# Cross-attention scores as three fp32r products, and another grouping of the FFN's columns with a ninth paired column, in a one-core decoder layer

## The chip, the cores and the metric

The kernel runs on one core of a Trainium2 chip. The metric is the device time of one execution in microseconds. Three runs of the kernel before gave 868.54, 869.44 and 870.27 us; the median is 869.44 us. Lower is better.

## What is computed

One layer of a causal decoder, for 512 prompt tokens and 8 samples of 4 tokens (544 token columns in all), model width 1024, all in fp32:

```python
gb, gc, u, q, k, v = split_mix(rmsnorm(x, norm_mix_w) @ w_in)       # conv mixer and differential attention
x += concat(conv_mixer, diff_attention) @ w_out
mk, mv = memory_kv(mem, norm_mem_w, w_ckv)                          # 256 memory tokens, 4 heads of 256
q = (rmsnorm(x, norm_cross_w) @ w_cq).reshape(b, t, 4, 256)
s = einsum('bqhd,bkhd->bhqk', q, mk) * 256 ** -0.5                  # the scores over the memory
x += einsum('bhqk,bkhd->bqhd', softmax(s), mv) @ w_co
up = rmsnorm(x, norm_ffn_w) @ w_up                                  # 1024 -> 2 * 2816: gate half and up half
c = causal_dwconv(up, prefix, conv_w, conv_b)                       # width 3, per channel
x += (silu(c[..., :2816]) * c[..., 2816:]) @ w_down                 # 2816 -> 1024
y = rmsnorm(x, norm_final_w)
```

## The kernel before

Activations lie transposed: 128 channels on the partitions, tokens along the row. `x` is 8 such k-tiles of 544 columns. An fp32 product is made of three fp32r products: each operand is split into a high part (ScalarE, a copy to fp32r) and a low part (VectorE, the operand minus its high part), and high x high, high x low and low x high are added in one PSUM bank. For weights these are `w_hi` (L1531, a ring of 3) and `w_lo` (L1867, a ring of 4, like the raw weights `w_raw` that the DMA brings, L870). The split of tile n + 3 can begin on ScalarE only when tile n is done (`split_hi`, L1524 to L1532), and the load of tile n + 4 is issued when tile n is done.

**A tile** is one block of 128 output channels: for `k` k-tiles, 3 matmuls for each half of 272 tokens, so 6 matmuls per k-tile (L1180). Its result lies in one of two PSUM pairs, `proj0` or `proj1` by the parity of its number, and tile n may start only when the result of tile n - 2 has been taken out (`wait_tile_out`, L1158).

**Order.** `make_schedule` (L164) writes one list of steps. Each engine walks the same list and issues its own part of each step, in that order, and an engine that waits in one step holds all its later steps up.

**Cross attention.** Eight query tiles (`cq`) fill `qc_t`. Then come eight units `c_score` (two pairs of heads by four token blocks). A unit is 4 matmuls of two fp32 operands, `mk_t` and `qc_t`, 128x256 each (L1431; the trace shows each as two instructions). VectorE takes the maximum (L2258), ScalarE the exponential (L1744), VectorE scales by the reciprocal (`c_mix`, L2265 and L2268), and TensorE transposes (`c_turn`, L1273), one unit behind the scores. Between them stand value tiles (L1136) and the sample group's work. The step `cq_blocks`, just behind the first `c_score`, concerns GpSimd alone.

**FFN.** There are 22 columns of 128 channels. An unpaired column is a gate tile and an up tile of 8 k-tiles each, 96 matmuls. A paired column computes both with 7 products (`prod`, r = 1, 2, 5, 6, 7, 3, 4, in that order) instead of 8, each 12 matmuls, 84 in all (L1262 to L1264); the weight sums that it needs are made on VectorE (`sums`, L2069 to L2073) and split in three parts (`pair_split`, L2082). Paired are 5, 7, ... 19, eight columns. For each column VectorE then scales (`up_in`, L2021), applies the convolution (`taps`; its first tap is ScalarE's, L1789, the other two L2030 and L2032), multiplies by the gate (`gate`, L2037, L2039), ScalarE splits off the high part (L1798) and VectorE the low part (`act`, L2043). Down tiles sum the columns of a group into `x` (`add`, L1999); the groups are columns 0-3, 4-7, 8-11, 12-15 and 16-21, and the down tiles of a group stand two each beside the first four columns of the next group. The last group's eight down tiles have 6 k-tiles each; the first two are begun (`half_tile`) with all k-tiles but the last. Behind each of them ScalarE squares the result and applies the final norm's weight, and VectorE adds the squares up. The last tile is done half by half (`last_half`), and the final norm follows.

In what follows d(g, n) is down tile n of the group g, counted from 0.

## Time and profile before

| | us |
|---|---|
| median of three runs | 869.44 |
| the profiled execution, its own time | 869.0 |
| the span of its trace | 867.2 |
| TensorE busy | 848.2 (98%) |
| VectorE busy | 553.9 (64%) |
| ScalarE busy | 364.2 (42%) |
| mean granted TensorE clock | 0.995 |

The span runs from the first to the last instruction; the profiled execution took 1.8 us more than it. TensorE's busy time counts a matmul until its modelled end, so consecutive matmuls overlap, and what one costs is read from the distance between the starts. L numbers are lines of the kernel.

### The profile page before, as it was taken

How to read it: one execution, taken by the hardware profiler on the slowest of the kernel's cores; microseconds unless marked ns; L12 is line 12 of the kernel's file. 1: busy time of each engine (PE TensorE's matmuls, PEld its weight loads, DVE VectorE, ACT ScalarE, POOL GpSimd, SP SyncE). 2: the span in 40 equal slices, each digit the busy share in tenths (PEclk: the TensorE clock that was granted, in tenths of full speed). 3: DMA queues.
4: the chain of work that ended last, by engine and by line, in shares of the span. 5: the costliest groups of instructions: out<-in, count | busy, mean ns of one | idle time of the engine just before them, and what ended most of it. 6: DMA issues, size and time to landing. Idle time of an engine off the chain costs nothing.

```text
span 867.2 us, 17354 instructions
## 1 busy us (share of the span) xinstructions
PE 848.2 (98%) x6884; PEld 798.8 (92%) x6884; DVE 553.9 (64%) x981; ACT 364.2 (42%) x652; POOL 76.9 (9%) x149
## 2 busy tenths in 40 slices
PE   7999999999999999999999999999999999999994
PEld 6988877789999999877899999999999999999994
DVE  6444246678584633465454899679688796796754
ACT  7302143366453711354333665345254353452452
POOL 2320000000000000000000331101012011010200
PEclk9999999999999999999999999999999999999998
DMA  8898699731233465579134222233223322332223
GB/s 309 264 366 293 211 328 328 243 99 43 57 99 119 149 243 180 184 282 375 49 114 133 87 74 73 85 105 95 86 82 89 120 75 84 112 96 66 77 73 104
DMA packets 50146, 131.25 MB, mean 151 GB/s; under 512 B 5939, under 2 KB 8503, under 8 KB 49810
## 3 DMA queue, kind: packets, MB, share of 16 engines
q1 hardware_dynamic: 48064, 124.40, 43.6%
q0 software_dynamic: 1712, 5.62, 1.8%
q8 instruction: 55, 0.90, 0.4%
q14 instruction: 25, 0.20, 0.1%
q10 hardware_dynamic: 290, 0.12, 0.1%
HBM read 123.12 MB, written 7.00 MB: 150 GB/s over the span
## 4 chain that ended last, share of the span: by engine, by line
PE 82%; DVE 1%; DMA 1%; issue 1%; ACT 0%; SPq 0%; DVEq 0%
PE proj L1180 53%; PE proj L1136 3%; PE proj L1197 2%; PE score L1264 2%; PE score L1263 2%; PE score L1262 2%; PE score L1431 2%; PE proj L1199 2%; PE proj L1198 2%; PE T L1264 1%; PE T L1263 1%; PE T L1262 1%; PE score L1397 1%; PE T L1273 1%; PE T L1416 1%; PE score L1466 1%
## 5 line engine op out<-in xcount | busy, mean ns | idle before, releaser
L1180 PE MATMUL proj<-a_hi,w_hi 128*128 128x272 f32 (+1 forms) x740 | 160.0, 291 | 6.3 <-DVE w_lo L1890 6.1
L1531 ACT ACTIVATE w_hi<-w_raw 128x1024 fp32r<-128x1024 f32 (+2 forms) x128 | 118.4, 931 | 111.8 <-PE proj L1180 85.0
L1180 PE MATMUL proj<-a_lo,w_hi 128*128 128x272 f32 (+1 forms) x740 | 158.4, 289 | 0.0
L1180 PE MATMUL proj<-a_hi,w_lo 128*128 128x272 f32 (+1 forms) x740 | 158.3, 288 | 0.0
L1867 DVE TENSOR_TENSOR w_lo<-w_raw,w_hi 128x1024 fp32r<-128x1024 f32 (+2 forms) x128 | 136.3, 1070 | 31.5 <-ACT w_hi L1531 31.4
L1180 PEld LDWEIGHTS proj<-a_hi,w_hi 128*128 128x128 f32 x740 | 118.5, 189 | 13.1 <-issue 6.7
L1180 PEld LDWEIGHTS proj<-a_lo,w_hi 128*128 128x128 f32 x740 | 118.9, 190 | 0.0
L1180 PEld LDWEIGHTS proj<-a_hi,w_lo 128*128 128x128 f32 x740 | 118.3, 190 | 0.0
L1180 PE MATMUL proj<-d_hi,w_hi 128*128 128x272 f32 x448 | 92.6, 288 | 0.0
L1180 PE MATMUL proj<-d_hi,w_lo 128*128 128x272 f32 x448 | 92.3, 288 | 0.0
L1180 PE MATMUL proj<-d_lo,w_hi 128*128 128x272 f32 x448 | 92.2, 288 | 0.0
L1789 ACT ACTIVATE conv<-up_pad,fvec 128x560 f32<-128x560 f32 x44 | 37.7, 858 | 109.2 <-DVE up_pad L2022 109.0
L1180 PEld LDWEIGHTS proj<-d_lo,w_hi 128*128 128x128 f32 x448 | 70.1, 188 | 0.0
L1180 PEld LDWEIGHTS proj<-d_hi,w_lo 128*128 128x128 f32 x448 | 69.9, 189 | 0.0
L1180 PEld LDWEIGHTS proj<-d_hi,w_hi 128*128 128x128 f32 x448 | 69.8, 188 | 0.0
L1112 POOL COPY f_state<-up_pad 128x18 f32<-128x18 f32 x44 | 35.2, 799 | 330.9 <-DVE up_pad L2022 330.9
L1999 DVE TENSOR_TENSOR x<-proj,x 128x544 f32<-128x544 f32 x39 | 28.1, 722 | 42.9 <-PE proj L1180 42.9
L1197 PE MATMUL proj<-a_hi,w_hi 128*128 128x272 f32 x160 | 48.1, 300 | 0.0
L1199 PE MATMUL proj<-a_hi,w_lo 128*128 128x272 f32 x160 | 46.2, 289 | 0.0
L1198 PE MATMUL proj<-a_lo,w_hi 128*128 128x272 f32 x160 | 46.1, 288 | 0.0
L2030 DVE SCALAR_TENSOR_TENSOR conv<-up_pad,fvec,conv 128x560 f32<-128x560 f32 x44 | 35.8, 813 | 9.6 <-ACT conv L1789 9.6
L2032 DVE SCALAR_TENSOR_TENSOR conv<-up_pad,fvec,conv 128x560 f32<-128x560 f32 x44 | 35.3, 803 | 1.6
(360 smaller groups left out, 1654.4 us busy)
## 6 DMA issues: line engine op xcount, KB each, us to landing
w_raw<-in_w_up SPq DMA_DIRECT2D x28, 512.0 KB, 3.6
w_raw<-in_w_in SPq DMA_DIRECT2D x21, 512.0 KB, 3.9
early_pages<-in_cache_k SPq DMA_DIRECT2D x32, 256.0 KB, 5.2
pages<-in_cache_v SPq DMA_DIRECT2D x32, 256.0 KB, 5.3
c_pages<-in_cache_mem_k SPq DMA_DIRECT2D x16, 512.0 KB, 6.6
c_pages<-in_cache_mem_v SPq DMA_DIRECT2D x16, 512.0 KB, 6.1
p_raw<-in_w_up SPq DMA_DIRECT2D x16, 512.0 KB, 4.0
w_raw<-in_w_down SPq DMA_DIRECT2D x32, 256.0 KB, 2.7
```

Source lines behind the costliest of these rows:

```text
L1112: pool.tensor_copy(f_state[:, j * FT + i, :].rearrange("p (b w) -> p b w", w=2), free_dims(pad, SEQ, [(6, 1 + DEC_BATCH), (1, 2)])).then_i ...
L1136: mm = pe.matmul(proj[part][:, rows, :], act[:, k, rows * P:(rows + 1) * P], wt.rearrange("p a b -> p (a b)"), start=(k == 0 and a == 0), ...
L1180: mm = pe.matmul(tile_banks(n)[:, half, 0:width], wt, act[:, at, half * HALF:half * HALF + width], start=(k == 0 and a == 0), stop=(k == w ...
L1197: pe.matmul(out, w_h, a_hi[:, k, cols], start=(k == 0), stop=False)
L1198: pe.matmul(out, w_h, a_lo[:, k, cols], start=False, stop=False)
L1199: mm = pe.matmul(out, w_l, a_hi[:, k, cols], start=False, stop=(k == KT - 1))
L1531: act.activation(w_hi[:, n % W_HI_RING, 0:kt, :], w_raw[:, n % W_RING, 0:kt, :], ACT.Copy).then_inc(w_hi_ready, 1)
L1789: act.activation(conv[:, j, 0:CONV], up_pad[:, j, i % 2, 0:CONV], ACT.Identity, bias=fvec[:, 6 * FT + n:6 * FT + n + 1], scale=fvec[:, n:n ...
L1867: dve.tensor_tensor(w_lo[:, n % W_RING, 0:kt, :], w_raw[:, n % W_RING, 0:kt, :], w_hi[:, n % W_HI_RING, 0:kt, :].bitcast(F32), ALU.subtrac ...
L1999: dve.tensor_tensor(held, out[:, :, 0:HALF], held, ALU.add).then_inc(tile_out[arg % 2], 1)
L2030: done(dve.scalar_tensor_tensor(out=out, in0=pad[:, 1:1 + CONV], scalar=fvec[:, 2 * FT + n:2 * FT + n + 1], in1=out, op0=ALU.mult, op1=ALU ...
L2032: dve.scalar_tensor_tensor(out=out, in0=pad[:, 2:2 + CONV], scalar=fvec[:, 4 * FT + n:4 * FT + n + 1], in1=out, op0=ALU.mult, op1=ALU.add) ...
```

## The change

Three things change.

The scores: `qc_t` and `mk_t` are split too, and a unit is 12 fp32r matmuls (L1473 to L1475 of the changed kernel) instead of 4 fp32 ones. ScalarE makes the high parts of a query tile in two copies of 256 columns, behind the next query tile (`query_hi`); the keys' high parts of heads 0 and 1 come in one copy of 1024, those of heads 2 and 3 in four copies of 256 (`keys_hi`). VectorE makes the low parts in the same pieces. The last query tile and the keys of heads 2 and 3 are split in the step `cq_blocks`, and VectorE's low parts of the keys wait for the copy of `mk_t` to DRAM, since they take its place.

The groups: the last six columns are now two groups, 16-18 and 19-21. The eight tiles of d(3, n) stand 2, 4 and 2 beside columns 16, 17 and 18, with 4 k-tiles each as before. The tiles d(4, n) have 3 k-tiles (18 matmuls); six of them stand beside columns 19, 20 and 21, two at a time, and d(4, 6) and d(4, 7) behind column 21. Then come the eight tiles d(5, n), with 3 k-tiles each. There are 48 down tiles instead of 40, with the same matmuls in all. In the last group the steps of tile f split the weights of tile f + 3, before f + 2.

The pair: column 21 becomes a ninth paired column.

```diff
 SELF_UNITS = SEQ // P * HEADS
-FFN_GROUPS = [range(0, 4), range(4, 8), range(8, 12), range(12, 16), range(16, 22)]
-PAIRED = list(range(5, 20, 2))
+FFN_GROUPS = [range(0, 4), range(4, 8), range(8, 12), range(12, 16), range(16, 19), range(19, 22)]
+PAIRED = list(range(5, 22, 2))
 DIST = 384
...
+DOWN_BESIDE = {4: (2, 4, 2), 5: (2, 2, 2)}
 def beside_of(i):
...
     g = next(g for g, group in enumerate(FFN_GROUPS) if i in group)
-    j = i - FFN_GROUPS[g][0]
-    return [(f"down{g - 1}", "add", n) for n in (2 * j, 2 * j + 1)] if g and j < 4 else []
+    if g == 0:
+        return []
+    counts, j = DOWN_BESIDE.get(g, (2, 2, 2, 2)), i - FFN_GROUPS[g][0]
+    first = sum(counts[:j])
+    return [(f"down{g - 1}", "add", n) for n in range(first, first + counts[j])]
...
             if i in PAIRED:
-                q = PAIRED.index(i)
-                order += [("prod", q, r) for r in (1, 2)] + beside[:1] + [("prod", q, r) for r in (5, 6)]
-                order += beside[1:] + [("prod", q, r) for r in (7, 3, 4)]
+                q, half = PAIRED.index(i), len(beside) // 2
+                order += [("prod", q, r) for r in (1, 2)] + beside[:half] + [("prod", q, r) for r in (5, 6)]
+                order += beside[half:] + [("prod", q, r) for r in (7, 3, 4)]
             else:
                 order += [("up", "gate", i), ("up", "up", i)] + beside
+    order += [(f"down{len(FFN_GROUPS) - 2}", "add", n) for n in range(sum(DOWN_BESIDE[len(FFN_GROUPS) - 1]), KT)]
     return order + [(LAST_DOWN, "add", n) for n in range(KT)]
...
                 s += [("pair_out", q, 1), ("pair_out", q, 2)]
-                if not beside_of(i):
-                    s += [("pair_hi", q, 1), ("pair_split", q, 1)]
             if r == 6:
...
             if r == 3:
-                s += [("pair_out", q, 7), ("pair_out", q, 3), ("up_in", i, 0)] + [("w_lo", late)] * bool(beside_of(i))
+                s += [("pair_out", q, 7), ("pair_out", q, 3), ("up_in", i, 0), ("w_lo", late)]
+                if i == FT - 1:
+                    s += [("w_hi", late + 1), ("w_lo", late + 1)]
             if r == 4:
-                s += [("taps", i, 0), ("pair_out", q, 4), ("pair_load", q + 1), ("up_in", i, 1), ("taps", i, 1), ("gate", i)]
-                s += [("sums", q + 1)] * (i + 2 in PAIRED) + [("act", i)]
+                s += [("taps", i, 0), ("pair_out", q, 4), ("pair_load", q + 1), ("up_in", i, 1), ("taps", i, 1)]
+                if i == FT - 1:
+                    s += [("w_hi", late + 2), ("w_lo", late + 2)]
+                s += [("gate", i)] + [("sums", q + 1)] * (i + 2 in PAIRED) + [("act", i)]
             continue
...
         if phase != "up":
-            q = FFN_ORDER[j - 1][1] if FFN_ORDER[j - 1][0] == "prod" else None
-            if q is not None and FFN_ORDER[j - 1][2] == 6:
+            before, behind = FFN_ORDER[j - 1], FFN_ORDER[j + 1]
+            if behind[0] == "prod" and behind[2] == 7:
                 late = f + 2
                 s += hi + [("add", f)]
+            elif before == ("prod", len(PAIRED) - 1, 4):
+                s.append(("add", f))
+            elif behind[0] == LAST_DOWN:
+                s += [("w_hi", f + 3), ("w_lo", f + 3), ("add", f)]
             else:
                 s += hi + lo + [("add", f)]
-                if q is not None:
-                    s += [("pair_hi", q, 1), ("pair_split", q, 1)]
-                if FFN_ORDER[j - 1][0] == "up":
-                    i = FFN_ORDER[j - 1][2]
-                    if i + 1 in PAIRED:
-                        s.append(("pair_split", PAIRED.index(i + 1), 2))
-                    s.append(("act", i))
+            if before[0] == "prod" and before[2] == 2:
+                s += [("pair_hi", before[1], 1), ("pair_split", before[1], 1)]
+            if before[0] == "up":
+                i = before[2]
+                if i + 1 in PAIRED:
+                    s.append(("pair_split", PAIRED.index(i + 1), 2))
+                s.append(("act", i))
             continue
...
             s.append(("norm", "up"))
-        if soon is not None and beside_of(i):
+        if soon is not None and i >= len(FFN_GROUPS[0]):
             after_hi, after_lo = split_next(f + 1)
...
         f = TILE[LAST_DOWN, "add", n]
-        hi, lo = split_next(f)
+        hi, lo = split_next(f + 1)
         s += [("tile", f)] + hi + lo + [("add", f)]
...
                 out = proj[LAST % 2][:, half, 0:cols.stop - cols.start]
-                for k in range(4) if part == 0 else range(4, kt):
+                for k in range(kt // 2 + 1) if part == 0 else range(kt // 2 + 1, kt):
                     w_h, w_l = w_hi[:, LAST % W_HI_RING, k, :], w_lo[:, LAST % W_RING, k, :]
...
                             wait_tile_out(pe, TILE["cq", "cq", d])
+                        pe.wait_ge(sem("pair_lo"), (MK_LO[0], MK_LO[1])[hp])
                     wait_empty(pe, uses[0])
                     for h2 in range(2):
+                        out = by_pages(bank["S1"][:, h2 * N_MEM:(h2 + 1) * N_MEM])
                         for d in range(2):
-                            mm = pe.matmul(bank["S1"][:, h2 * N_MEM:(h2 + 1) * N_MEM],
-                                           block_cols(qc_t, 2 * (2 * hp + h2) + d, i),
-                                           mk_t[:, 2 * (2 * hp + h2) + d, :], start=(d == 0), stop=(d == 1))
+                            n = 2 * (2 * hp + h2) + d
+                            q_h, q_l = qc_hi(n, i // 2)[:, (i % 2) * P:(i % 2 + 1) * P], block_cols(qc_lo, n, i)
+                            pe.matmul(out, q_h, mk_hi(n), start=(d == 0), stop=False)
+                            pe.matmul(out, q_h, by_pages(mk_lo[:, n, :]), start=False, stop=False)
+                            mm = pe.matmul(out, q_l, mk_hi(n), start=False, stop=(d == 1))
                     mm.then_inc(full["S1"], 1)
...
+            def query_hi(d):
+                wait_tile_out(act, TILE["cq", "cq", d])
+                for half in range(2):
+                    hi = act.activation(qc_hi(d, half), qc_t[:, d, half * (HALF + HALF_S):half * (HALF + HALF_S) + HALF_P], ACT.Copy)
+                hi.then_inc(sem("pair_hi"), 1)
+            def keys_hi(part):
+                wait_tile_out(act, TILE["mem", "mem", KT - 1])
+                if part:
+                    act.wait_ge(tile_done, TILE["cq", "cq", KT - 1] + 1)
+                    for d in range(4, KT):
+                        hi = act.activation(mk_hi(d), by_pages(mk_t[:, d, :]), ACT.Copy)
+                else:
+                    hi = act.activation(norm_split[:, 2560:2560 + 4 * N_MEM].rearrange("p (a b) -> p a b", b=N_MEM),
+                                        mk_t[:, 0:4, :], ACT.Copy)
+                hi.then_inc(sem("pair_hi"), 1)
             def rstd_of(out, in_, width_scale):
...
                     split_hi(arg)
+                elif kind == "cq_blocks":
+                    query_hi(KT - 1)
+                    keys_hi(1)
                 elif kind == "tile":
...
                         split_hi(arg + 2)
+                    if TILES[arg]["kind"] == "cq":
+                        if TILES[arg]["i"]:
+                            query_hi(TILES[arg]["i"] - 1)
+                        else:
+                            keys_hi(0)
                     w = TILES[arg]
...
+            def query_lo(d):
+                dve.wait_ge(sem("pair_hi"), d + 2)
+                for half in range(2):
+                    cols = slice(half * (HALF + HALF_S), half * (HALF + HALF_S) + HALF_P)
+                    lo = dve.tensor_tensor(qc_lo[:, d, cols], qc_t[:, d, cols], qc_hi(d, half).bitcast(F32), ALU.subtract)
+                lo.then_inc(sem("pair_lo"), 1)
+            def keys_lo(part):
+                dve.wait_ge(sem("mk_saved"), 16)
+                dve.wait_ge(sem("pair_hi"), (1, KT + 2)[part])
+                if part:
+                    for d in range(4, KT):
+                        lo = dve.tensor_tensor(by_pages(mk_lo[:, d, :]), by_pages(mk_t[:, d, :]), mk_hi(d).bitcast(F32),
+                                               ALU.subtract)
+                else:
+                    held = norm_split[:, 2560:2560 + 4 * N_MEM].rearrange("p (a b) -> p a b", b=N_MEM)
+                    lo = dve.tensor_tensor(mk_lo[:, 0:4, :], mk_t[:, 0:4, :], held.bitcast(F32), ALU.subtract)
+                lo.then_inc(sem("pair_lo"), 1)
             def split_lo(n):
...
                     split_lo(arg)
+                elif kind == "cq_blocks":
+                    query_lo(KT - 1)
+                    keys_lo(1)
                 elif kind == "add":
...
                                                  ).then_inc(tile_out[arg % 2], 1)
+                        if w["i"]:
+                            query_lo(w["i"] - 1)
+                        if w["i"] == 3:
+                            keys_lo(0)
                     if w["kind"] in ("k", "v"):
```

The first place is VectorE's queue in cross attention, from the maximum of the first score unit to the scaling of its exponentials (`c_mix`). Before (the row ahead of it is the last query tile's):

```order
L2108 SCALAR_TENSOR_TENSOR qc_t<-proj1,rstd 128x544 [waits tile_done]
L2258 TENSOR_REDUCE c_small<-score 128x2 [waits full_S1]
L1867 TENSOR_TENSOR w_lo<-w_raw,w_hi 128x1024 [waits w_hi_ready]
L2265 RECIPROCAL c_small<-c_small 128x2 [waits free_S1]
L2268 TENSOR_SCALAR norm_area<-norm_area,c_small 128x256 [waits dve_step]
```

And now (`qc_lo` and `mk_lo` are the low parts of queries and keys):

```order
L2355 TENSOR_REDUCE c_small<-score 128x2 [waits full_S1]
L1936 TENSOR_TENSOR qc_lo<-qc_t,a_hi 128x256 [waits pair_hi]
L1936 TENSOR_TENSOR qc_lo<-qc_t,a_lo 128x256
L1945 TENSOR_TENSOR mk_lo<-mk_t,c_keys_hi 128x256 [waits pair_hi,mk_saved]
L1945 TENSOR_TENSOR mk_lo<-mk_t,c_keys_hi 128x256
L1945 TENSOR_TENSOR mk_lo<-mk_t,c_keys_lo 128x256 x2
L1957 TENSOR_TENSOR w_lo<-w_raw,w_hi 128x1024 [waits w_hi_ready]
L2362 RECIPROCAL c_small<-c_small 128x2 [waits free_S1]
L2365 TENSOR_SCALAR norm_area<-norm_area,c_small 128x256 [waits dve_step]
```

Six subtractions now stand between the maximum and the weight split, and so ahead of the reciprocal and of the scaling, for which the first transpose waits.

The second place is VectorE's queue in the FFN's last column, from the scaling of its up half to the first down tile's addition (`x<-proj0,x`). Before, where column 21 is unpaired and the addition is that of d(4, 0):

```order
L2022 TENSOR_TENSOR up_pad<-proj1,rstd 128x8x4
L1867 TENSOR_TENSOR w_lo<-w_raw,w_hi 128x768 [waits w_hi_ready]
L2030 SCALAR_TENSOR_TENSOR conv<-up_pad,fvec,conv 128x560 [waits fvec_loaded,first_tap]
L2032 SCALAR_TENSOR_TENSOR conv<-up_pad,fvec,conv 128x560 [waits dve_step]
L2037 TENSOR_TENSOR gated<-conv 128x2x256 [waits conv_ffn_done,silu_done]
L2039 TENSOR_TENSOR gated<-conv 128x32
L2043 TENSOR_TENSOR a_lo<-gated,a_hi 128x544 [waits tile_done,act_hi]
L1867 TENSOR_TENSOR w_lo<-w_raw,w_hi 128x768 [waits w_hi_ready]
L1999 TENSOR_TENSOR x<-proj0,x 128x544 [waits tile_done]
```

And now, where column 21 is paired and the first two additions are those of d(4, 6) and d(4, 7):

```order
L2115 TENSOR_TENSOR up_pad<-y_pair,rstd 128x8x4
L2123 SCALAR_TENSOR_TENSOR conv<-up_pad,fvec,conv 128x560 [waits fvec_loaded,first_tap]
L2125 SCALAR_TENSOR_TENSOR conv<-up_pad,fvec,conv 128x560 [waits dve_step]
L1957 TENSOR_TENSOR w_lo<-w_raw,w_hi 128x384 [waits w_hi_ready]
L2130 TENSOR_TENSOR gated<-conv 128x2x256 [waits conv_ffn_done,silu_done]
L2132 TENSOR_TENSOR gated<-conv 128x32
L2136 TENSOR_TENSOR a_lo<-gated,a_hi 128x544 [waits tile_done,act_hi]
L2092 TENSOR_TENSOR x<-proj0,x 128x544 [waits tile_done]
L1957 TENSOR_TENSOR w_lo<-w_raw,w_hi 128x384 [waits w_hi_ready]
L2092 TENSOR_TENSOR x<-proj1,x 128x544 [waits tile_done]
```

Before, TensorE had d(4, 0) and d(4, 1) to work on without one of these additions. Now the additions of d(4, 6) and d(4, 7) stand behind the whole convolution and gating of column 21, and TensorE's d(5, 0) and d(5, 1) go to the PSUM pairs that these additions free.

## Rows read from the trace of the kernel before

**Rows 1.** the page's first part: engine, busy us, share, instructions.

```profile
PE 848.2 (98%) x6884; PEld 798.8 (92%) x6884; DVE 553.9 (64%) x981; ACT 364.2 (42%) x652; POOL 76.9 (9%) x149
```

**Rows 2.** TensorE's waits: waiting, awaited, us in total, times, longest.

```profile
PE proj L1180 <- DVE w_lo L1890: 6.1, 1, 6.1
...
PE proj L1180 <- DVE x L1999: 0.2, 1, 0.2
```

**Rows 3.** timeline of TensorE in a memory-key tile: start, length, instruction.

```profile
292.01 0.28 PE L1180 MATMUL proj<-a_lo,w_hi 128*128 128x256 f32 x1
...
293.79 0.28 PE L1180 MATMUL proj<-a_lo,w_hi 128*128 128x256 f32 x1
```

**Rows 4.** timeline around the fifth score step.

```profile
374.71 1.89 PE L1431 MATMUL score<-mk_t,qc_t 128*128 128x256 f32 x8
...
376.44 0.60 PE L1273 MATMUL T<-ident,norm_area 128*128 128x128 f32 x4
```

**Rows 5.** timeline from the first score step to the first transpose.

```profile
353.65 0.47 ACT L1744 ACTIVATE norm_area<-score,c_small 128x256 f32<-128x256 f32 x1
...
354.10 1.05 ACT L1531 ACTIVATE w_hi<-w_raw 128x1024 fp32r<-128x1024 f32 x1
...
355.18 1.23 DVE L1867 TENSOR_TENSOR w_lo<-w_raw,w_hi 128x1024 fp32r<-128x1024 f32 x1 [2.03 <-ACT w_hi L1531]
...
356.52 0.62 DVE L2268 TENSOR_SCALAR norm_area<-norm_area,c_small 128x256 f32<-128x256 f32 x2
...
357.98 0.60 PE L1273 MATMUL T<-ident,norm_area 128*128 128x128 f32 x4
```

**Rows 6.** groups by form, ACT and DVE: instructions and their mean ns.

```profile
L1621 ACT ACTIVATE a_hi<-norm_area 128x256 fp32r<-128x256 f32 x8 | 3.3, 418 | 7.0 <-DVE norm_area L1956 7.0
...
L1950 DVE TENSOR_TENSOR a_lo<-norm_area,a_hi 128x256 fp32r<-128x256 f32 x8 | 3.4, 421 | 0.2
...
L1867 DVE TENSOR_TENSOR w_lo<-w_raw,w_hi 128x512 fp32r<-128x512 f32 x32 | 21.3, 685 | 0.0
```

**Rows 7.** the chain that ended last, in order of time, in the FFN.

```profile
690.18 17.97 PE proj L1180 x144
...
745.72 3.01 PE proj L1180 x24
751.75 3.00 PE proj L1180 x24
```

**Rows 8.** timeline behind a paired column (11), ScalarE and VectorE.

```profile
690.27 0.85 ACT L1789 ACTIVATE conv<-up_pad,fvec 128x560 f32<-128x560 f32 x1 [6.22 <-DVE up_pad L2022]
...
696.94 0.18 DVE L2039 TENSOR_TENSOR gated<-conv 128x32 f32<-128x32 f32 x1
```

**Rows 9.** timeline behind the last column (21).

```profile
822.99 0.72 DVE L2043 TENSOR_TENSOR a_lo<-gated,a_hi 128x544 fp32r<-128x544 f32 x1 [0.73 <-ACT a_hi L1798]
...
826.01 0.72 DVE L1999 TENSOR_TENSOR x<-proj,x 128x544 f32<-128x544 f32 x1 [1.33 <-PE proj L1180]
...
826.88 0.49 PE L1180 MATMUL proj<-a_hi,w_hi 128*128 128x272 f32 x2 [0.16 <-DVE x L1999]
```

**Rows 10.** DMA issues: instruction, count, KB each, median us to landing.

```profile
w_raw<-in_w_down SPq DMA_DIRECT2D x32, 256.0 KB, 2.7
```

**Rows 11.** timeline of TensorE's first matmuls.

```profile
6.73 0.66 PE L1180 MATMUL proj<-a_lo,w_hi 128*128 128x272 f32 x2
...
9.97 0.41 PE L1180 MATMUL proj<-a_hi,w_hi 128*128 128x272 f32 x2
```

**Rows 12.** windows: each engine's busy us, then granted clock, at the end.

```profile
855.00:860.00 5.00, 1.29 (x5) 0.44 (x4) 4.85 (x6) 1.70 (x4) 0.00 (x0) 0.92 0.45 161
860.00:867.20 7.20, 0.00 (x0) 0.00 (x0) 0.65 (x2) 0.00 (x0) 0.00 (x0) 0.50 0.58 198
```

**Rows 13.** timeline of the end.

```profile
849.51 0.29 PE L1214 MATMUL proj<-a_hi,w_hi 128*128 128x272 f32 x1
...
855.51 2.20 DVE L2323 TENSOR_TENSOR x<-x,rstd 128x1088 f32<-128x1088 f32 x2
```

23 lines of the change are left out of this document (21 added, 2 removed).

## The prediction, made before the changed kernel was run

> **What bounds the kernel now.** I read the page's busy times first. TensorE is busy for 848.2 of 867.2 us [rows 1], so the question is whether it ever stands still. The list of its waits answers that: 6.1 us once, before the first weights are split, and for the rest fractions of a microsecond, the one in the FFN 0.2 us [rows 2]. So removed matmuls count in full, and each wait of TensorE that the change brings counts in full too. VectorE is busy 553.9 us, 64% [rows 1], but its queue is in order, so what matters is how late one instruction stands in it. For that I read the timeline at the two places where the order moves, the first score unit and the end of the last FFN column.
>
> **The scores, removed and added.** A fp32 unit starts at 374.71 and the transposes behind it at 376.44 [rows 4]: 1.73 us. Of fp32r matmuls with 256 columns in one bank, 15 lie between 292.01 and 293.79 [rows 3], 0.119 us each; 12 take 1.43 us. That is 0.30 less, 8 x 0.30 = 2.4 us. I take -2.3; bounds -2.5 and, if the strided operands cost 0.01 us a matmul, -1.4.
>
> **The splits beside the query tiles** cost nothing. A query tile has 48 matmuls, as the unpaired tiles have, 144 of which take 17.97 us [rows 7]: 6 us. VectorE gets two subtractions of 256 columns more (0.42 us each [rows 6]) and ScalarE two copies (0.42). The one piece of 1024 on each is as long as a weight split, 1.23 and 1.05 us [rows 5]. Both engines otherwise have a weight split and at most one more instruction in those 6 us.
>
> **The first score unit** does cost. Before, ScalarE ends its exponentials at 353.65 + 0.47 = 354.1, and splits the next weights up to 355.15, VectorE theirs from 355.18 to 356.4, then come the reciprocal and the scaling up to 357.14; the transpose starts at 357.98 [rows 5], without waiting, 0.84 us later. Now the exponentials end 0.3 us earlier, at 353.8, and six copies stand behind them: back to back some 0.35 us each from 0.42 [rows 6], so up to 355.9. VectorE's last four subtractions wait for all of them: 355.9 + 4 x 0.38 = 357.4. Then its weight split (1.2, to 358.6) and 0.75 for reciprocal and scaling: 359.3. TensorE comes to the transpose after two shorter units, 357.98 - 0.6 = 357.4, and goes on at about 359.5: +2.1 us. Later units keep their distance, since VectorE's work for a unit is what it was. Bounds: 0.8, if copies and subtractions pass at 0.25 us, and 3.2, if they take 0.42 each and each handover 0.1 more.
>
> **The ninth pair.** 12 of 96 matmuls go. An unpaired one takes 17.97 / 144 = 0.125 us; between two down tiles, 745.72 to 751.75, lie 24 products and one tile of 3.01 us [rows 7], so a product matmul takes 3.02 / 24 = 0.126. So 96 x 0.125 - 84 x 0.126 = 12.0 - 10.6: -1.4 us (bounds -1.5, -1.3). The regrouping leaves the number of down matmuls alone. It adds 8 additions of 0.72 us [rows 9] to VectorE, and smaller, more frequent tiles: with 3 k-tiles one takes 18 x 0.125 = 2.25 us instead of 3.0 or 4.5.
>
> **The end of the last column** costs most. Call Z the moment at which TensorE ends the last product of column 21. It has d(4,6) and d(4,7), 4.5 us of work, and then d(5,0) must wait for the addition of d(4,6). In VectorE's queue that addition stands behind all of column 21. How long this is shows behind column 11, which is paired too: its last product ends at 690.18 [rows 7], ScalarE's first tap starts at 690.27, the gated product is ready at 696.94 + 0.18 = 697.1 [rows 8]: 6.95 us. To this comes one weight split of 384 columns between taps and gate, 0.5 (256 take 0.42 and 512 take 0.69 [rows 6]); then 0.73 us for ScalarE's high part and 0.72 for the low part, as at 822.99 [rows 9]; then the addition, 0.7; then 0.15, as between 826.73 and 826.88 [rows 9]. Together Z + 9.7 against Z + 4.5: TensorE waits 5.2 us. Bounds 4.4 and 5.9.
>
> **The clock.** The first matmuls of the kernel, after 6.1 us of standing still, are twice as far apart (0.45 us for two, row 6.73) as those from 9.97 on (0.25) and go on so for 3 us [rows 11], and behind the last matmul the granted clock falls from 0.92 in one stretch to 0.50 in the next [rows 12], which is 1.2 GHz. So I expect that after 5.2 us without work the next matmuls run at 1.2 GHz for some 3 us, which costs half of that where TensorE is what is late: +1.3 us; bounds 0 and 2.5. The Trainium skill ("TensorE: Matmul & The Clock Gate", Part 1) says the same, that the half clock is the resting state and activity releases it; by that rule the term stands, without it the sum would be lower by it.
>
> **The down tiles behind it.** In the last group the weight split of tile f + 3 now stands before the addition of f, on VectorE, and it waits for ScalarE's split, which waits until tile f is done and its weights have landed. So behind the end of tile f come (lengths estimated from those of 256 and 512 columns [rows 6]) 0.25 for the handover, 0.55, 0.5 and the addition 0.7, with 0.15 to TensorE: 2.15 to 2.35 us, as much as tile f + 1 lasts (2.25). The load helps nothing: 2.7 us for 256 KB [rows 10], issued when f - 1 is done, lands within 0.5 us of f's end. For d(5,2) it is worse. d(5,0) and d(5,1) are begun together, so the end of d(5,0) is only 0.75 us before d(5,2) is due, and 2.2 are needed: 1.45 us. The change of ScalarE's table and the first squares then come in one tile's time: 0.2 and 0.8 us at d(5,3) and d(5,4). Together 2.45, less the 0.2 that stood there before: +2.3 us. Bounds 0.5 and 4.5.
>
> **The very end.** The last tile starts at 849.51 and the final scaling at 855.51 [rows 13], 6.0 us. The last tile is 2.25 us shorter, but that gain is counted in the matmuls already. The time to the final scaling shrinks by less. Before the first half's norm the addition of the last tile but one, its square and two sums of squares must pass, four steps of about 0.7 us with handovers of 0.1 to 0.2, then the first half's own addition and square, 0.45 each with theirs: 3.1 + 1.2 = 4.3 us and the norm's own 1.0. Of the 6.0 us, which 2.25 fewer would make 3.75, about 4.9 to 5.0 remain: an estimate from these lengths, +1.2 us; bounds 0 and 1.8.
>
> **Columns 16 to 20.** Column 17 gets two down tiles more, which gives VectorE time. Beside columns 19 and 20 two tiles shrink from 3.0 to 2.25 us each while VectorE's work falls by 0.13 per split. I count no wait, and up to 1.5 us in the range.
>
> **The sum.** -2.3 + 2.1 - 1.4 + 5.2 + 1.3 + 2.3 + 1.2 = +8.4 us, on the profiled execution's own 869.0 us (867.2 of span and 1.8 around it): 877.4. That execution lay 0.4 us below the median of 869.44, so 877.5 is my value, rounded between the two ways of adding.
>
> **Rivals.**
> First, the clock stays up in the wait: the same waits at 2.4 GHz, without 1.3 us, 876.2. For it: at the very end the clock fell only some time after the last matmul, and the wait may be 4.4. Against it: a 6 us gap is followed by the low clock at the start.
> Second, VectorE is late through the whole of columns 18 to 21, not only behind 21, because 8 additions and the shorter tiles come there: 1.5 us before column 21 and 2 more in the last group, 881. For it: the small distances reckoned above. Against it: 64% over the whole, and TensorE waited only 0.2 us in all of the FFN [rows 2].
> Third, the other side: VectorE frees d(4,6)'s pair in time. The point is Z + 4.5 us. If the addition is out by then, the wait, the low clock and the wait of d(5,2) all go, and with them the late end; -2.3 + 2.1 - 1.4 leaves -1.6, or 867.8, and 865.7 if the first transpose waits for nothing either. For it: the matmuls saved are sure. Against it: the queue order and the 6.95 us of column 11, of which nothing is taken away.
> Fourth, the waits are there but half as long, because ScalarE and VectorE overlap better than behind column 11 and the end takes up the rest: 872.5.
>
> **Chances.** The forecast 0.50, the first rival 0.18, the second 0.12, the third 0.10, the fourth 0.10. The forecast's own range, from its terms, is 874.5 to 880.5. The range I give, 872.0 to 881.0, leaves out the third rival and the far part of the second. A measurement can tell 0.2%, 1.7 us, from no change. Faster by more is most of the third rival, 0.08; within 0.2% the rest of it and a little of the fourth, 0.04; slower 0.88.
>
> **What would show it.** In the profile after: a score unit of 1.43 us; one wait of about 2 us of the first transpose for the scaling, and none like it at the later seven; 84 matmuls in column 21; in the list of TensorE's waits one entry of about 5 us of a down tile for VectorE's addition, and a second of about 1.5 for the tile two later; matmuls 0.45 us per two behind the long one. The forecast is wrong if d(5,0) starts within a microsecond of the end of d(4,7), or if TensorE waits in columns 18 to 21.

## The result and the profile after

The changed kernel takes 880.23 us (median of 4 runs, 879.92 to 882.80), the kernel before, beside it, 869.11 (4 runs). The ratio is 1.0127, with a 95% interval of 1.0113 to 1.0141: slower by 11 us. The forecast was 877.5 with a range of 872.0 to 881.0 and 0.88 for slower. The profiled execution took 879.92 us with a span of 878.1, 10.9 more than before.

First the busy times on its page, to be read against [rows 1].

```profile
PE 848.1 (97%) x6904; PEld 799.5 (91%) x6904; DVE 572.0 (65%) x1026; ACT 374.8 (43%) x686; POOL 76.8 (9%) x149
```

TensorE is busy for as long as before, 848.1 us. It does less work in that time, but some of it at half the clock, and the profile counts that as busy. The 10.9 us therefore have to be looked for in waits and in rates. TensorE's list of waits (engine and line, what it waited for, us in total, times, longest), where [rows 2] had 0.2 us for an `x` and nothing else outside the start and the end:

```profile
PE proj L1218 <- issue: 4.9, 1, 4.9
PE proj L1218 <- DVE x L2092: 1.8, 2, 1.2
PE T L1311 <- DVE norm_area L2365: 1.7, 1, 1.7
...
PE proj L1218 <- DVE up_pad L2115: 0.3, 1, 0.3
PE score L1508 <- DMA c_pages<-in_cache_mem_k: 0.2, 1, 0.2
```

The entry of 4.9 us names no releaser ("issue"); the timeline below shows which it was. The first score unit and what stands behind it (start, length, engine, line, instruction, count, idle time before it and its releaser), answering to [rows 4, 5]:

```profile
350.65 0.28 PE L1473 MATMUL score<-norm_split,a_hi 128*128 128x256 f32 x1
...
352.06 0.62 PE L1174 MATMUL proj<-w_hi,a_hi 128*128 128x512 f32 x2
...
356.63 0.76 DVE L1945 TENSOR_TENSOR mk_lo<-mk_t,c_keys_lo 128x256 fp32r<-128x256 f32 x2
...
357.30 1.22 DVE L1957 TENSOR_TENSOR w_lo<-w_raw,w_hi 128x1024 fp32r<-128x1024 f32 x1
...
358.63 0.62 DVE L2365 TENSOR_SCALAR norm_area<-norm_area,c_small 128x256 f32<-128x256 f32 x2
...
359.30 0.66 PE L1311 MATMUL T<-ident,norm_area 128*128 128x128 f32 x4 [1.70 <-DVE norm_area L2365]
```

The unit lies between 350.65 and 352.06, 1.41 us instead of 1.73. The transpose comes at 359.30 where it came at 357.98 (8.65 us behind the first unit's start instead of 7.45), after 1.70 us of waiting for the scaling; ahead of the scaling stand `keys_lo` (355.95 to 357.3) and a weight split. The later units wait for no scaling. Before, the first unit began 0.12 us earlier:

```profile
350.53 1.89 PE L1431 MATMUL score<-mk_t,qc_t 128*128 128x256 f32 x8
```

FFN work starts at 475.33 us; it was 475.34 before. So this stage gains 0.1 us and no more.

The end of column 21, answering to [rows 8, 9]. The first row is TensorE's last product; the moment called Z in the prediction is 830.24.

```profile
830.12 0.29 PE L1302 MATMUL score<-d_hi,t_lo 128*128 128x272 f32 x1
...
835.64 0.80 DVE L2125 SCALAR_TENSOR_TENSOR conv<-up_pad,fvec,conv 128x560 f32<-128x560 f32 x1
836.36 0.55 DVE L1957 TENSOR_TENSOR w_lo<-w_raw,w_hi 128x384 fp32r<-128x384 f32 x1
836.83 0.68 DVE L2130 TENSOR_TENSOR gated<-conv 128x512 f32<-128x512 f32 x1
...
838.34 0.72 DVE L2136 TENSOR_TENSOR a_lo<-gated,a_hi 128x544 fp32r<-128x544 f32 x1 [0.72 <-ACT a_hi L1867]
838.98 0.72 DVE L2092 TENSOR_TENSOR x<-proj,x 128x544 f32<-128x544 f32 x1
839.62 0.55 DVE L1957 TENSOR_TENSOR w_lo<-w_raw,w_hi 128x384 fp32r<-128x384 f32 x1
...
839.80 0.80 PE L1218 MATMUL proj<-a_hi,w_hi 128*128 128x272 f32 x2 [4.89 <-issue]
...
840.39 0.66 PE L1218 MATMUL proj<-a_lo,w_hi 128*128 128x272 f32 x2
```

d(4,6) and d(4,7) end at 834.75. VectorE takes the taps, a weight split, the gate and the low part, and only then, at 838.98, adds d(4,6), which had been ready since 832.5. That addition ends at 839.70, and d(5,0), which needs the PSUM pair that it frees, starts at 839.80, 5.05 us after d(4,7)'s end; so the wait listed under "issue" is the one for VectorE's addition. Its first pairs of matmuls are 0.45 us apart, not 0.25. The same stretch by windows (each engine's busy us with its count, then the granted clock, the DMA share and GB/s), to compare with [rows 12]:

```profile
836.00:840.00 4.00, 0.20 (x1) 0.23 (x2) 3.28 (x7) 1.07 (x2) 0.00 (x0) 0.84 0.34 100
840.00:842.00 2.00, 2.00 (x10) 2.00 (x11) 0.80 (x2) 0.00 (x0) 0.00 (x0) 0.50 0.00 0
...
844.00:846.00 2.00, 2.00 (x12) 2.00 (x12) 0.00 (x0) 0.00 (x0) 0.00 (x0) 0.61 0.00 0
846.00:848.00 2.00, 1.12 (x10) 0.91 (x8) 0.97 (x2) 0.53 (x1) 0.00 (x0) 1.00 0.22 51
```

The granted clock is 0.50, which is 1.2 GHz, at the first matmul behind the wait and until 845.5 us; by the windows of 2 us it fell at about 838.7, still in the wait. Twelve pairs take 5.58 us instead of 3.0. The last group and the end, answering to [rows 13]:

```profile
847.03 0.56 DVE L1957 TENSOR_TENSOR w_lo<-w_raw,w_hi 128x384 fp32r<-128x384 f32 x1 [6.23 <-ACT w_hi L1573]
...
848.37 0.49 PE L1218 MATMUL proj<-a_hi,w_hi 128*128 128x272 f32 x2 [1.25 <-DVE x L2092]
...
853.70 0.49 PE L1218 MATMUL proj<-a_hi,w_hi 128*128 128x272 f32 x2 [0.53 <-DVE x L2092]
...
860.54 0.29 PE L1252 MATMUL proj<-a_hi,w_hi 128*128 128x272 f32 x1
...
865.66 1.29 DVE L2420 TENSOR_TENSOR x<-x,rstd 128x1088 f32<-128x1088 f32 x1 [0.24 <-ACT rstd L1909]
```

d(5,2) waits 1.25 us at 848.37 and d(5,4) 0.53 at 853.70, each for an addition that stands behind a split. From the last tile's start at 860.54 to the final scaling at 865.66 are 5.12 us (6.0 before). After that come 12.44 us to the end of the span instead of 11.69.

### The profile page after: what moved, and what is told of

Same layout as the page of the kernel before. It is cut to its first block, busy times and chain, and to the rows that moved or that the text cites. A ratio compares the mean times of both kernels' runs of the same rounds, so it can differ in the third digit from the quotient of the medians.

```text
span 878.1 us, 17516 instructions
## 1 busy us (share of the span) xinstructions
PE 848.1 (97%) x6904; PEld 799.5 (91%) x6904; DVE 572.0 (65%) x1026; ACT 374.8 (43%) x686; POOL 76.8 (9%) x149
## 4 chain that ended last, share of the span: by engine, by line
PE 77%; DVE 4%; ACT 2%; issue 2%; DMA 1%; DVEq 0%; SPq 0%; ACTq 0%
PE proj L1218 49%; PE proj L1235 2%; PE proj L1174 2%; PE score L1302 2%; PE score L1301 2%; PE score L1300 2%; PE proj L1237 2%; PE proj L1236 2%; PE T L1302 2%; PE T L1301 2%; PE T L1300 2%; PE score L1435 1%; PE T L1454 1%; PE T L1311 1%; DMA c_pages<-in_cache_mem_k 1%
## 5 line engine op out<-in xcount | busy, mean ns | idle before, releaser
L1218 PE MATMUL proj<-a_hi,w_hi 128*128 128x272 f32 (+1 forms) x746 | 162.5, 292 | 13.3 <-DVE w_lo L1980 6.2
L1218 PE MATMUL proj<-a_lo,w_hi 128*128 128x272 f32 (+1 forms) x746 | 160.4, 290 | 0.0
L1218 PEld LDWEIGHTS proj<-a_hi,w_lo 128*128 128x128 f32 x746 | 120.2, 191 | 0.0
L1218 PE MATMUL proj<-d_hi,w_hi 128*128 128x272 f32 x416 | 85.9, 287 | 0.0
L1218 PE MATMUL proj<-d_lo,w_hi 128*128 128x272 f32 x416 | 85.5, 287 | 0.0
L1218 PE MATMUL proj<-d_hi,w_lo 128*128 128x272 f32 x416 | 85.5, 288 | 0.0
L1218 PEld LDWEIGHTS proj<-d_lo,w_hi 128*128 128x128 f32 x416 | 65.0, 188 | 0.0
L1218 PEld LDWEIGHTS proj<-d_hi,w_lo 128*128 128x128 f32 x416 | 64.8, 188 | 0.0
L1218 PEld LDWEIGHTS proj<-d_hi,w_hi 128*128 128x128 f32 x416 | 64.8, 188 | 0.0
L2092 DVE TENSOR_TENSOR x<-proj,x 128x544 f32<-128x544 f32 x47 | 33.8, 720 | 32.7 <-PE proj L1218 32.7
```

Source lines behind the costliest of these rows:

```text
L1218: mm = pe.matmul(tile_banks(n)[:, half, 0:width], wt, act[:, at, half * HALF:half * HALF + width], start=(k == 0 and a == 0), stop=(k == w ...
```

## The experiments

Each kernel ran in five rounds beside the kernel before on the same chip, in three sets, 1 to 4, 5 to 8 and 9 to 12 (the first on one chip, the other two on another); the kernel before had medians of 870.13, 869.72 and 870.09 us in them. Ratios are to that kernel, with their 95% intervals. The edits of experiments 1 to 4 are shown in short form.

**Experiment 1, the scores alone.** The kernel before with the parts of the change that touch the cross attention, so in its unit:

```diff
-  mm = pe.matmul(out, qc_t, mk_t, ...)                        # fp32, once for each d
+  pe.matmul(out, q_h, mk_hi(n)); pe.matmul(out, q_h, mk_lo); mm = pe.matmul(out, q_l, mk_hi(n))
```

> The kernel before, with only the cross attention of the change: twelve fp32r products of 256 columns in place of four fp32 ones of 256, and their splits. The FFN is that of before. My theory, from the trace after the change: eight units save 0.3 us each (2.4), the first transpose waits 1.7, and the keys of the second group of samples, which land at 392.3 us, take 0.2 to 0.7 more, so the ratio lies between 0.999 and 1.000 (-0.7 to 0 us) and the FFN begins at 475.3 us as before. Rival: the stage does gain and something in the FFN of the changed kernel hid it; then this kernel is 2.3 us faster (0.9974). Second rival: the splits cost something elsewhere, and it is slower by 1 us or more.

869.91 us, ratio 1.0000 (0.9991 to 1.0008). In its profile the first transpose waits 1.7 us and lies 1.65 us later than before, the six units behind it win 0.27 us each, and the FFN begins at 475.37. Of the 1.65 us, 0.6 were there already when the first unit started (351.14 against 350.53), so counted from that start the stage is 0.6 us shorter than before, which is within the interval of the times. The keys of the second group are not waited for, so my remark on them explains nothing: the late first transpose takes back most of the gain.

**Experiment 2, the FFN alone.** The kernel before with the groups, the ninth pair and the step list of the change:

```diff
-FFN_GROUPS = [..., range(12, 16), range(16, 22)];  PAIRED = list(range(5, 20, 2))
+FFN_GROUPS = [..., range(12, 16), range(16, 19), range(19, 22)];  PAIRED = list(range(5, 22, 2))
```

> The kernel before, with only the FFN of the change: groups of 4, 4, 4, 4, 3 and 3 columns and the ninth pair. The scores are in fp32 as before. My theory: all of the loss is here, +10.9 us (ratio 1.0125, range 1.0115 to 1.0135), with one wait of about 4.9 us in front of the first down tile of the last group. Rival: part of the loss comes from the scores (a state of queues or loads that lasts into the FFN), and this kernel loses less than 10 us.

881.30 us, ratio 1.0133 (1.0115 to 1.0150). All of the loss is in the FFN, and the 4.9 us entry is there. In this execution the matmuls behind it ran at the low rate for 3.2 us (840.24 to 843.42), not 5.6, which cost 1.4 us instead of 2.6: the same wait, another price.

**Experiment 3, two additions moved in VectorE's queue.**

```diff
-  taps(21,0), ..., up_in(21,1), taps(21,1), w_lo d(5,1), gate 21, act 21, add d(4,6), ..., add d(4,7)
+  taps(21,0), ..., up_in(21,1), add d(4,6), taps(21,1), add d(4,7), w_lo d(5,1), gate 21, act 21
```

> The changed kernel, where only the places of two additions in the step list differ: those of d(4,6) and d(4,7) stand before the second taps and before the gate of column 21 instead of behind its activation. My theory, the order of VectorE's queue makes the wait: TensorE ends d(4,7) at 834.75 and begins d(5,0) at once; then the last products of d(5,0), for which it needs the gated column 21, wait some 2 us (the low part is ready at about 839.8 instead of 839.05, the two begun tiles end at 837.9). The long wait goes from 4.9 to 1.5-2.5 us, and the low clock with most or all of its 2.6 us; against the changed kernel -3 to -6 us, so about 875 us, +4.5 to +7.5 on the kernel before. Rival, the wait is for column 21's own chain and not for the bank: TensorE stands still as long, only one step later, and less than 1 us is gained.

874.83 us, ratio 1.0062 (1.0048 to 1.0077), 5.7 us less than the changed kernel's ratio gives. VectorE's additions and TensorE's restart in its timeline:

```profile
833.70 0.72 DVE L2097 TENSOR_TENSOR x<-proj,x 128x544 f32<-128x544 f32 x1
...
836.42 0.72 DVE L2097 TENSOR_TENSOR x<-proj,x 128x544 f32<-128x544 f32 x1
837.06 0.55 DVE L1962 TENSOR_TENSOR w_lo<-w_raw,w_hi 128x384 fp32r<-128x384 f32 x1
...
837.66 0.52 PE L1223 MATMUL proj<-a_hi,w_hi 128*128 128x272 f32 x2 [1.19 <-DVE w_lo L1962]
...
839.91 0.49 PE L1223 MATMUL proj<-a_hi,w_hi 128*128 128x272 f32 x2 [0.47 <-DVE a_lo L2141]
```

The additions now lie at 833.70 and 836.42. TensorE waits 1.19 us for the weight split of the next tile and 0.47 for the low part of column 21, 1.7 us in place of 4.9, and between 834 and 846 us the clock is 1.00 in every window. So the order of the queue made the long wait, as predicted.

**Experiment 4, the wait filled.** 36 matmuls between d(4,7) and d(5,0) that nothing reads.

```diff
+  s += [("filler",)]
...
+  elif kind == "filler":
+      ...
+      wait_pair_out(pe, q, 4)
+      for _ in range(36):
+          pe.matmul(bank[pair_bank(q, 4)][:, 0:HALF], ones[:, :], split_sums[:, 1, 0:HALF], start=True, stop=True)
```

> The changed kernel, with 36 further matmuls of 272 columns in the wait before the first down tile of the last group; they write a bank that is not in use and nothing reads them. They take 36 x 0.125 = 4.5 of the 4.9 us. My theory: the low clock is brought on by the standing still, so the 24 matmuls behind the wait take 3.0 us instead of 5.6, and this kernel is 2.6 us faster than the changed one (877.6 us, ratio 1.0098) although it does more. Rival: the low rate has another cause (the switch to the new group's operands, the load of the chip as a whole), the 24 matmuls take 5.6 us as before and the time stays at 880.2. Second rival: the slow matmuls delay nothing that VectorE would not delay by itself; then they are fast but the time moves by less than 1 us.

878.04 us, ratio 1.0094 (1.0079 to 1.0108). The filler, and the first two rows behind it, then the windows:

```profile
835.06 4.61 PE L1343 MATMUL score<-split_sums,ones 128*128 128x272 f32 x36
840.12 0.49 PE L1219 MATMUL proj<-a_hi,w_hi 128*128 128x272 f32 x2 [0.46 <-issue]
840.46 0.41 PE L1219 MATMUL proj<-a_lo,w_hi 128*128 128x272 f32 x2
```

```profile
840.00:842.00 2.00, 1.88 (x15) 1.91 (x16) 1.12 (x3) 0.00 (x0) 0.00 (x0) 1.00 0.00 0
842.00:844.00 2.00, 2.00 (x18) 2.00 (x18) 0.00 (x0) 0.00 (x0) 0.00 (x0) 1.00 0.00 0
```

The starts behind the wait are 0.34 and then 0.25 us apart, and the clock stays at 1.00. The kernel does more and takes 2.9 us less (1.0127 against 1.0094). The low rate comes from the standing still, and the time lost by it (2.6 us in the profile) reaches the end of the kernel whole.

**Experiment 5, column 21 not paired.** The changed kernel with

```diff
-PAIRED = list(range(5, 22, 2))
+PAIRED = list(range(5, 20, 2))
-                s += [("w_hi", f + 3), ("w_lo", f + 3), ("add", f)]
+                s += hi + lo + [("w_hi", f + 3), ("w_lo", f + 3), ("add", f)]
```

> The changed kernel with the groups of 4, 4, 4, 4, 3 and 3 kept, but column 21 multiplied out as two ordinary tiles; d(4,4) to d(4,7) stand behind them. My theory: the long wait needs both, the regrouping and the pair; without the pair column 21's work on VectorE is over before d(4,6) ends, so the wait of 4.9 and the low clock's 2.6 us go and 12 more matmuls cost 1.4: 874.0, between 872.5 and 876, still 3 to 6 us slower than the kernel before, because d(5,2) and d(5,4) wait (1.25 and 0.5 us) and the end is as late as in the changed kernel. Rival: the regrouping alone makes the wait, so it stays above 4 us and the time above 879.

880.44 us, ratio 1.0121 (1.0106 to 1.0136). My number failed by 6 us. The long wait did fall from 4.9 to 1.29 us, but it was not alone; the list shows five waits of the same kind:

```profile
PE proj L1218 <- DVE x L2092: 6.0, 5, 2.0
```

The longest, 1.96 us at 817.12, is new. It lies at the start of column 21. A split of 1024 columns for the column's own tiles (815.12, 1.22 us) now stands in VectorE's queue ahead of the addition for which TensorE waits (816.25 to 816.97); a second one (817.52) stands ahead of the next addition, for which nothing waits. The windows around it:

```profile
812.00:816.00 4.00, 3.16 (x26) 2.94 (x24) 3.24 (x6) 2.90 (x5) 0.23 (x2) 1.00 0.46 157
816.00:820.00 4.00, 2.88 (x18) 2.91 (x19) 3.37 (x5) 1.25 (x2) 0.00 (x0) 0.83 0.20 53
820.00:824.00 4.00, 4.00 (x27) 4.00 (x26) 0.00 (x0) 0.00 (x0) 0.00 (x0) 0.74 0.00 0
```

The clock falls after less than 2 us of standing still, from 818.7 to 822.1 us, and 96 matmuls take 13.74 us instead of 12. Without the pair the long splits come back, and I take it that the shorter tiles of the small groups leave VectorE no time for them; that was not tried by itself. So the regrouping loses with the pair and without it, at different places.

**Experiment 6, the pair without the regrouping.** The kernel before with

```diff
-PAIRED = list(range(5, 20, 2))
+PAIRED = list(range(5, 22, 2))
```

> The kernel before with a ninth pair in column 21 and its own groups of 4, 4, 4, 4 and 6 columns. Behind the last product stand the two down tiles that are begun for columns 16 to 20, 2 x 3.75 = 7.5 us, before anything needs column 21, which is ready some 8.5 us behind the last product (6.95 to the gated product, 0.73 and 0.72 for its parts). My theory: TensorE waits 1 us or less and no bank is waited for, so the pair's 1.4 us are kept in part: -0.4 us, between -1.2 and +0.7 (ratio 0.9986 to 1.0008). Rival: the pair itself brings the loss, since VectorE and ScalarE are late behind it whatever follows; then there is a wait of more than 2 us behind column 21 and the time is over 871.

877.16 us, ratio 1.0088 (1.0075 to 1.0101). Behind column 21 the wait is 1.0 us, as reckoned. But the waits list has one that I had not looked for, ahead of the column:

```profile
PE score L1262 <- DVE p_lo L2082: 5.3, 1, 5.3
PE proj L1180 <- DVE a_lo L2043: 1.0, 1, 1.0
PE score L1262 <- ACT y_pair L1826: 0.6, 1, 0.6
```

```profile
810.10 1.22 DVE L2082 TENSOR_TENSOR p_lo<-p_raw,p_hi 128x1024 fp32r<-128x1024 f32 x1
...
811.38 0.60 PE L1262 MATMUL score<-d_hi,p_hi 128*128 128x272 f32 x1 [5.27 <-DVE p_lo L2082]
```

Column 20 has no down tile beside it. VectorE comes to the low part of the pair's weights only at 810.10, and TensorE has by then stood still for 5.27 us (and the 12 matmuls behind it take 2.9 instead of 1.5 us, up to 814.3, at the low rate). So the rival was right about the time and wrong about the place: not behind the column, but ahead of it.

**Experiment 7, the late split.** Experiment 1, with query 7 and the keys of heads 2 and 3 split behind the first unit's scaling.

```diff
-            s.append(("c_mix", *units[0]))
+            s += [("c_mix", *units[0]), ("split_rest",)]
...
-                elif kind == "cq_blocks":     # on ScalarE and on VectorE: the split of query 7 and keys 4 to 7
+                elif kind == "split_rest":
```

> The kernel of the first experiment (scores in fp32r, FFN of before), where the split of query 7 and of the keys of heads 2 and 3 stands behind the first unit's scaling instead of ahead of its exponentials; only the fifth unit needs them. My theory: the first transpose's wait of 1.7 us goes, and what the matmuls save comes out: -1.3 us against the kernel before (-1.9 to -0.6, ratio about 0.9985). Rival: the keys of the second group of samples, for which the changed kernel waited 0.2 us at 392.3 us with the DMA engines 93 to 102% busy, land no earlier; then TensorE waits for them instead and less than 0.6 us is left.

868.09 us, ratio 0.9980 (0.9970 to 0.9990): 1.7 us faster than the kernel before, and clear of experiment 1's interval.

**Experiment 8, all additions first.** Experiment 3, and for every tile of the last group

```diff
-        s += [("tile", f)] + hi + lo + [("add", f)]
+        s += [("tile", f), ("add", f)] + hi + lo
```

> The kernel of the third experiment (additions of d(4,6) and d(4,7) early), where besides in the last group each addition stands ahead of the split of the next weights instead of behind it. My theory, the short waits of the last group come from the queue too: the wait of d(5,2) falls from 1.25 to some 0.4 us and that of d(5,4) (0.5) goes, 1.0 to 1.6 us less than the third experiment's 874.8: about 873.5. Rival: the splits, now later, are waited for instead (three k-tiles last 2.25 us, the weights land as late as before), and the time stays within 0.5 us or grows.

873.83 us, ratio 1.0045 (1.0033 to 1.0057), 1.5 us less than experiment 3 by the ratios, though their intervals overlap. The waits of down tiles for an addition, 1.8 us in two before, are 0.7 in two. Most of them too came from the queue.

**Experiment 9, the seventh once more.** The same kernel, without an edit. It ran on the chip of experiment 7, and not on another one as the expectation says.

> The kernel of the seventh experiment once more, on another chip, since its profiled execution was the longest of its eight (870.1 against a median of 868.09) and so shows another wait than the others have. My theory: again 1 to 2.5 us faster than the kernel before (ratio 0.9975 to 0.999), and a representative profile shows no wait for a scaling in the score units and the FFN beginning at 473.5 to 474.5 us instead of 475.3. Rival: the gain was an accident of that set of runs; the ratio's interval then holds 1.

868.24 us, ratio 0.9981 (0.9970 to 0.9992). Its chain of waits (start, length, what) and two entries of its list of waits:

```profile
356.71 0.44 PE T L1298 x4
...
396.45 0.44 PE T L1298 x4
...
400.15 10.04 DMA c_pages<-in_cache_mem_v
410.24 0.62 PE score L1514
```

```profile
PE T L1298 <- DVE norm_area L2383: 0.7, 1, 0.7
PE score L1514 <- DMA c_pages<-in_cache_mem_v: 0.6, 1, 0.6
```

The first transpose starts at 356.71, 1.4 us earlier than in the chain of before (358.14), and no transpose waits for the scaling of a score unit (the 0.7 us are for a copy of the sample group). But 0.8 of the 1.4 us were there ahead of the stage, whose first unit starts at 349.77 instead of 350.53. Counted from that unit the first transpose comes after 6.78 us; before it was 7.45, in experiment 1 8.65. So the late split does take the wait away. At 396.45 the transposes are 2.3 us earlier than before (398.73), 1.5 counted from the unit. Then the DMA of value pages takes 10.04 us and ends the wait at 410.24, and 0.7 us are left. The FFN begins at 474.70, not at 473.5 to 474.5 as I had expected; that is 124.93 us behind the first unit, and 124.81 in the profile of before. In this execution the page loads took back all that the stage had gained. The time of both sets is nevertheless 1.7 to 1.8 us below the kernel before. So the gain in time is shown, and where it arises is not.

**Experiment 10, all three orders in the changed kernel.** The edits of experiments 3, 7 and 8 together.

> The changed kernel with all three orders altered: the late split of the seventh experiment, the early additions of the third and those of the eighth. My theory: the parts add, since they lie in different stages; 873.8 less 1.6 = 872.2 us, ratio 1.0025 to 1.004, so the changed FFN stays slower than that of before although no wait of more than 1.3 us is left in it: the rest lies behind the last down tile, where less product time hides the same work of VectorE, and in some small waits. Rival: the parts do not add (the late splits meet the same queue), and it is no faster than the eighth experiment.

872.55 us, ratio 1.0026 (1.0014 to 1.0039), where the ratios of experiments 8 and 7 together give 1.0026. The parts add. The mended FFN of the change is still 4.3 us behind the FFN of before (872.55 against 868.24).

**Experiment 11, half of the wait filled.** Experiment 4 with

```diff
-      for _ in range(36):
+      for _ in range(18):
```

> The changed kernel with 18 further matmuls instead of 36 at the start of the wait before the first down tile of the last group: 2.3 of the 4.9 us are filled and about 2.6 us of standing still are left. It is to show how the loss of clock goes with the length of the wait. My theory: standing still for 2.6 us brings the clock down as 2 us in column 21 of the fifth experiment did (0.83 and 0.74 in the stretches behind it), so the time is between the changed kernel's and that of the filled wait: 878.0 to 880.2, some 1.0 to 2.6 us of low clock left. Rival: half the wait costs nothing, and the time equals that of the fully filled wait within 0.3 us, with 3.0 us for the 24 matmuls.

879.69 us, ratio 1.0106 (1.0089 to 1.0122), between the changed kernel and experiment 4, though the intervals overlap with both. In its profile 2.67 us of standing still are left; the pairs behind them are 0.45 us apart from 840.37 to 843.09, which costs 1.6 us.

**Experiment 12, tiles beside column 20.** Experiment 6 with

```diff
-    return [... for n in (2 * j, 2 * j + 1)] if g and j < 4 else []
+    counts = (1, 2, 1, 2, 2, 0) if g == 4 else (2, 2, 2, 2)
```

> The kernel of the sixth experiment (groups of before, ninth pair in column 21), with the eight down tiles of group 3 laid beside columns 16 to 20 as 1, 2, 1, 2 and 2 instead of 2, 2, 2, 2 and 0. It is to show whether the wait of 5.3 us before column 21's first product (for the low part of its pair's weights) came from column 20's having no down tile beside it. My theory: yes; two tiles give 6 us, the wait goes and with it the low clock behind it (12 matmuls in 2.9 instead of 1.5 us), while the 0.6 and the 1.0 us inside and behind column 21 stay: 877.2 less 6 to 7.5, so about 870.4 (869.5 to 871.5), no faster than the kernel before. Rival: the pair's splits are late whatever stands beside column 20, or columns 16 and 18 with one tile each now wait, and the time stays above 873.

873.19 us, ratio 1.0035 (1.0023 to 1.0048). The waits:

```profile
PE score L1264 <- DVE p_lo L2084: 1.3, 2, 0.7
PE proj L1182 <- DVE a_lo L2045: 1.0, 1, 1.0
PE score L1264 <- ACT y_pair L1828: 0.6, 1, 0.6
```

The 5.3 us are gone, and the clock is 1.00 in every window from 770 to 840 us, so the missing tiles were the cause. My sum was 2.8 us too low, and the rival's second half came true: columns 16 and 18, with one tile each, now make the pairs of 17 and 19 wait (0.65 us at 740.75, 0.61 at 773.15). VectorE is busy for 9.83 of the 10 us from 770 on, and again from 800 on, where TensorE waits 0.4 us more, at 811.65. The rest of the 2.8 us is not accounted for.

## Why the prediction held, and where its sizes were off

**The scores.** Removed matmuls: 0.30 a unit predicted, 0.32 in the first and 0.27 to 0.31 in the others measured. First transpose 2.1 us later than it need be: it waited 1.70. That the split ahead of the scaling makes this wait is shown by experiment 9, where it is gone. Net -0.2 forecast, 0.0 measured (experiment 1, within 0.8 us). A profile can't tell more: in the seven traces with these scores in this order the stage, from its first unit to the FFN, is between 0.6 us shorter and 1.0 us longer than in the trace of before.

**The ninth pair and the long wait.** 12 matmuls went (-1.4). The wait was put at 5.2 us and took 5.05; the reading of column 11 [rows 7, 8] carried over, and the whole chain came out within 0.2 us. Experiment 3 shows the cause. Experiments 6 and 12 add what the prediction took for granted: the pair also needs down tiles ahead of it, and the last column can have them only on one side.

**The clock.** The mechanism was right (experiment 4), the size was not: 1.3 us forecast, 2.6 measured in the profile of the changed kernel, just beyond the upper bound of 2.5. I took one length for the low rate from the start of the kernel (3 us), where only the distances show it; the trace gives a granted clock of 1.00 there. Behind the waits of the other traces the matmuls ran at the low rate for 2.9 us after 5.3 of standing still (experiment 6), 3.4 after 2.7 (11), 3.4 after 2.0 (5), 3.2 after 4.9 (2) and 5.6 after 4.9 (the changed kernel), at a cost of 1.4, 1.6, 1.7, 1.4 and 2.6 us. By the windows the granted clock was low for 3.4 us in each of the first four and for 6.8 in the last (838.7 to 845.5), 1.1 of them still in the wait. Why it was low twice as long there, no run shows. This term, the cost of the low rate behind the wait, is the one that the sum had mis-sized.

**The down tiles behind it.** 1.45 at d(5,2) and 0.8 at d(5,4) forecast; 1.4 and 0.7 between the starts measured, 0.2 at d(5,3) not seen. +1.9 against +2.3. Experiment 8 shows that it is the queue.

**The very end.** 4.9 to 5.0 us from the last tile to the scaling forecast, 5.12 measured: +1.37 against +1.2. Not foreseen: from the start of VectorE's last scaling to the end of the span are 7.8 us, before 7.05. It is so in every kernel with the groups of 3 and 3. Only the last output's DMA lies there. In the changed kernel the DMA share falls from 0.66 to 0.07, about one engine of 16, at 874.25, and stays there until 874.95; in the kernel before it goes to 0 at once (864.1). The list of the DMA queues has one packet of instructions (q14, 0.01 MB) between the first store's issue and that end in the changed kernel and none in the kernel before. All 14 traces agree: one packet in experiments 3, 4, 5, 8, 10 and 11 (7.7 to 7.8 us), two in experiment 2 (8.9 us), none in 1, 6, 7, 9 and 12 (7.1 us). So the load of instructions that falls among the stores goes with the loss; no experiment moved it, and why it falls there stays open.

**Columns 16 to 20.** One wait of 0.3 us at d(4,3), in the range of 0 to 1.5. Word for word it is one of the signs by which the forecast was to be wrong (TensorE waits in columns 18 to 21); it is too small to carry the second rival.

The ledger by the changed kernel's profile: 0.0 - 1.4 + 0.3 + 5.05 + 2.6 + 1.9 + 1.4 + 0.75 = 10.6 of 10.9 us. The forecast's sum was 8.4; the clock (+1.3) and the end of the span (+0.75) are most of the difference. The measured 880.2 lies in the range by 0.8 us only: nearly every size that was off was off to the same side, and the range held because its upper end had been set high. Of the rivals the first (clock stays up) is refuted by the windows, the third (bank free in time) by the 5.05 us. The second, VectorE late through columns 18 to 21, gave 881, nearer to the measured time than my 877.5, but its mechanism is not in the profile: columns 18 to 20 wait 0.3 us in all. It is what happens when the pair is taken out (experiment 5).

## What to carry to other kernels

An instruction that frees a buffer for the engine that sets the time belongs ahead of work in its queue that nobody waits for: two moved additions returned half of the loss, and a split moved behind one scaling turned a change of no effect into a gain of 0.2%, in two sets of runs. The tail of a column of dependent work must be covered by as much independent work of TensorE as it is long; saving matmuls where the cover is short costs the wait and then the clock as well. And a gap of TensorE is to be priced with the low rate behind it, which here cost 1.4 to 2.6 us for gaps of 2.0 to 5.3 us and nothing for gaps of 1.2 us.

## What the runs showed of the hardware

- Standing still for 1.96 us (experiment 5) brought TensorE's granted clock to 0.50 about 1.6 us after it had gone on at full rate; gaps of 1.2 us (experiments 3 and 8) left it at 1.00, as did the two of 1.2 and 1.3 us in experiment 5 itself. The Trainium skill ("TensorE: Matmul & The Clock Gate", Part 1) says that the half clock is the resting state and that activity releases it. These rows agree with that, and they add that the clock can still fall when the engine is already at work again.
- After the same wait of 4.9 us in the same place the low rate lasted 5.6 us in one kernel and 3.2 us in another.
- An fp32 product of 256 columns costs as much as 3.7 fp32r products of them: 1.73 us for 4, 1.41 for 12.
- Where a packet of instructions was loaded while the last output was being stored, one DMA engine of 16 was busy for 0.7 us longer than the others (DMA share 0.07), and the end of the span came 0.7 us later (7 traces; two packets, 1.8 us, in one more).
